# Computing only the chosen experts, with two indirect row gathers for each chosen slot

## The chip, the cores and the metric

The kernel runs on one core of a Trainium2 chip; the other cores are idle. The metric is the device time of one execution in microseconds. The core has a matrix engine (TensorE, PE), a vector engine (DVE), an activation engine (ACT), a general engine (GpSimd, POOL) and SyncE (SP), each with its own instruction queue. Data come from the chip's memory by DMA over 16 DMA engines; SP and POOL issue the transfers here.

## The reference

One layer of an image trunk over 512 latent and 256 context tokens of width 2048, all in fp32: modulation, a token mixer (RG-LRU and RWKV7 halves), a residual with layer norm, and then a PEER mixture of 16,384 experts with a second residual and layer norm. The change touches what follows the mixer:

```python
def peer(h, w_q, sub_keys, u, v):        # u, v: [16384, 2048]
    q = (h @ w_q).reshape(B_, T, 8, 2, 128)
    s = einsum('bthpd,hpkd->bthpk', q, sub_keys)
    s1, i1 = top_k(s[..., 0, :], 16);  s2, i2 = top_k(s[..., 1, :], 16)
    cand_s = s1[..., :, None] + s2[..., None, :]       # 256 per head
    cand_i = i1 * 128 + i2
    top_s, pos = top_k(cand_s, 16);  idx = cand_i[pos]
    gates = softmax(top_s)
    # 8 heads x 16 = 128 chosen experts for each token
    act = gelu(einsum('nkd,nd->nk', u[idx], h))
    return einsum('nk,nkd->nd', gates * act, v[idx])

x = layer_norm(ALPHA * x + gt1 * o_lat, ln1_g, ln1_b)
f = peer(modulate(x, sh2, sc2), ...)
x = layer_norm(ALPHA * x + gt2 * f, ln2_g, ln2_b)
```

## The kernel before, in words

The program is a row of blocks; at the end of each all engines meet, so nothing of one block overlaps the next: `modulation`, `in_projection`, `rglru`, `rwkv`, and `tail` with `out_projection` (its layer norm included), `queries`, `route`, `experts`, `final`. Activations are kept feature-major: a tile has 128 features as partitions and 512 tokens along the row, 16 tiles for the width.

`out_projection` (L1421) ends with a layer norm (L1353) whose matrix product with a constant sums over features on PE. Its finish writes the modulated input of the experts as two fp32r parts, `h_hi` and `h_lo`, and SP stores the normed residual to `x1_dram` in four parts of 1 MB (L1459). `queries` (L1490) leaves, for every token, the 16 best keys and their scores for each of the 16 half-heads in `best_key` and `best_val`.

`route` (L1538) loops over four tiles of 128 tokens. DVE adds the pairs of scores to 256 candidates per head, finds the best 16, works out the two key indices and the softmax gates (L1648 to L1672). Then the chosen gates are spread to a dense matrix: for four tokens at a time DVE builds one-hot rows (L1685), POOL multiplies one of them by the gates (L1581), PE multiplies the two (L1603), ACT copies the product out (L1625), and SP stores 8 MB per tile to `gates_dram` (L1570).

`experts` (L1692) computes all 16,384 experts for all 512 tokens. The work goes in 16 groups of 16 units; a unit is a weight tile of 1 MB, first 8 of the table u, then 8 of the table v. SP loads a unit as soon as both conversions of the tile two units before are done (L1721); ACT makes the high part `ex_hi` (L1738), DVE the low part `ex_lo` (L1752); PE multiplies high by high, high by low and low by high (L1798), 48 matmuls a unit. After each u unit ACT applies Gelu (L1743), DVE multiplies by the gates (L1759) that POOL loads (L1728), and splits the result (L1761, L1763). After each v unit DVE adds two products of 128x512 into the sum `f` (L1769). There are two buffers of each tile.

`final` (L1823) reloads x1 (L1833), scales by the second gate (L1838), adds the residual (L1845) and runs the second layer norm with PE sums (L1378, L1382), ACT's root (L1392, L1394) and SP's four stores (L1854).

Elsewhere in the program, and named by the prediction: `modulation` loads eight weight tiles of 4 MB (L109); `rglru` loads 64 tiles of 1 MB from POOL's queue into three buffers (L479); `rwkv_scan` multiplies by an identity matrix on PE (L1075) to turn tiles.

## Time and profile before

| | |
|---|---|
| median of 3 runs (lowest to highest) | 6884.99 us (6883.69 to 6888.27) |
| the profiled execution's span | 6879.0 us |
| instructions | 80488 |
| PE, DVE, ACT, POOL busy | 6061.1, 2778.5, 1685.7, 366.5 us |
| read from memory, written | 531.84 MB, 61.09 MB |

The profiled execution has no time of its own beside its span; the runs' median stands 6 us above that span. Busy time counts an engine's instructions, not its waits. A granted clock of 1.00 is TensorE at 2.4 GHz and 0.50 at 1.2 GHz; between them a stretch holds both. A DMA share of 1.00 means that all 16 DMA engines had packets all the time. An fp32 matmul of the program stands in the trace as two records, an fp32r one as one.

### The profile page before, as it was taken

What the parts mean: (1) busy time and instruction counts of PE and PEld (TensorE: products, weight loads), DVE (VectorE), ACT (ScalarE), POOL (GpSimd) and SP (SyncE); (2) the same over time, 40 slices, a digit from 0 to 9 for tenths busy, and PEclk for the clock granted to TensorE, in tenths of its full rate; (3) what the DMA queues carried; (4) which work ended last, traced back from release to release, by engine and by line L of the source; (5) the groups of instructions that cost most, each with busy time, mean ns of one, the idle gap of its engine ahead of it and who ended that gap; (6) DMA issues with size and microseconds to landing.
All of it is one profiled execution on the core that took longest, in us unless ns stands there. A gap on an engine that the chain in (4) does not pass through costs nothing. (4 is left out here: it accounts for less than half of the span.)

```text
span 6879.0 us, 80488 instructions
## 1 busy us (share of the span) xinstructions
PE 6061.1 (88%) x32312; PEld 4951.1 (72%) x32312; DVE 2778.5 (40%) x3717; ACT 1685.7 (25%) x1951; POOL 366.5 (5%) x426
## 2 busy tenths in 40 slices
PE   6798988699999999959664569999999999999997
PEld 1687855687788877837453458888888888888885
DVE  1333433443433444232579933333333333333333
ACT  0111225333332333222213312222222222222222
POOL 0000010000000000010003400000000000000000
PEclk8899999788887888769887789999999999999998
DMA  5222275100000000031204353333333333333332
GB/s 227 91 86 82 102 250 182 41 21 11 11 8 8 21 11 11 1 109 61 98 31 79 67 144 110 110 106 107 110 110 110 105 108 108 110 110 106 107 108 86
DMA packets 199453, 595.47 MB, mean 87 GB/s; under 512 B 16884, under 2 KB 121972, under 8 KB 146292
## 3 DMA queue, kind: packets, MB, share of 16 engines
q1 hardware_dynamic: 176160, 477.24, 21.2%
q0 software_dynamic: 22976, 115.63, 5.0%
q8 instruction: 135, 2.21, 0.1%
q14 instruction: 34, 0.28, 0.0%
q10 hardware_dynamic: 148, 0.10, 0.0%
HBM read 531.84 MB, written 61.09 MB: 86 GB/s over the span
## 5 line engine op out<-in xcount | busy, mean ns | idle before, releaser
L1798 PE MATMUL ex_u<-h_hi,ex_hi 128*128 128x512 f32 x2048 | 797.6, 389 | 52.5 <-DVE ex_lo L1752 52.5
L1798 PE MATMUL ex_u<-h_lo,ex_hi 128*128 128x512 f32 x2048 | 797.4, 389 | 0.0
L1798 PE MATMUL ex_u<-h_hi,ex_lo 128*128 128x512 f32 x2048 | 797.3, 389 | 0.0
L1798 PE MATMUL ex_v<-ex_w_hi,ex_hi 128*128 128x512 f32 x2048 | 796.7, 389 | 0.0
L1798 PE MATMUL ex_v<-ex_w_lo,ex_hi 128*128 128x512 f32 x2048 | 796.7, 389 | 0.0
L1798 PE MATMUL ex_v<-ex_w_hi,ex_lo 128*128 128x512 f32 x2048 | 796.7, 389 | 0.0
L1738 ACT ACTIVATE ex_hi<-ex_raw 128x2048 fp32r<-128x2048 f32 x256 | 490.3, 1915 | 1100.8 <-PE ex_v L1798 1100.3
L1752 DVE TENSOR_TENSOR ex_lo<-ex_raw,ex_hi 128x2048 fp32r<-128x2048 f32 x256 | 586.5, 2291 | 84.1 <-ACT ex_hi L1738 84.1
L1769 DVE TENSOR_TENSOR f<-f,ex_v 128x512 f32<-128x512 f32 x256 | 164.5, 684 | 843.1 <-PE ex_v L1798 843.1
L1798 PEld LDWEIGHTS ex_u<-h_hi,ex_hi 128*128 128x128 f32 x2048 | 384.9, 188 | 132.7 <-DVE ex_lo L1752 52.7
L1759 DVE TENSOR_TENSOR ex_w<-ex_act,ex_gates 128x512 f32<-128x512 f32 x128 | 88.7, 693 | 882.2 <-ACT ex_act L1743 882.2
L1798 PEld LDWEIGHTS ex_u<-h_hi,ex_lo 128*128 128x128 f32 x2048 | 384.8, 188 | 80.0
L1798 PEld LDWEIGHTS ex_u<-h_lo,ex_hi 128*128 128x128 f32 x2048 | 384.8, 188 | 79.8
L1798 PEld LDWEIGHTS ex_v<-ex_w_hi,ex_lo 128*128 128x128 f32 x2048 | 384.4, 188 | 79.9
L1798 PEld LDWEIGHTS ex_v<-ex_w_lo,ex_hi 128*128 128x128 f32 x2048 | 384.4, 188 | 79.8
L1798 PEld LDWEIGHTS ex_v<-ex_w_hi,ex_hi 128*128 128x128 f32 x2048 | 384.4, 188 | 79.7
L1743 ACT ACTIVATE ex_act<-ex_u 128x512 f32<-128x512 f32 x128 | 76.8, 600 | 1077.3 <-PE ex_u L1798 1077.3
L994 DVE TENSOR_TENSOR rw_X<-rw_bank,rw_level_mask 128x512 f32<-128x512 f32 x240 | 164.4, 691 | 398.3 <-PE rw_bank L1110 396.9
L250 PE MATMUL pb_acc<-x_hi,pb_hi 128*128 128x512 f32 x832 | 213.0, 338 | 72.8 <-DVE pb_lo L221 72.8
L1685 DVE TENSOR_TENSOR rt_hot<-rt_iota,rt_sel 128x512 f32<-128x512 f32 x256 | 259.1, 1088 | 7.8 <-ACT rt_sel L1617 7.8
L1603 PE MATMUL rt_g<-rt_gated,rt_hot 128*128 128x128 f32 x1024 | 186.1, 339 | 86.2 <-POOL rt_gated L1581 85.2
L605 PE MATMUL late_acc<-lru_late_w,cond_act 128*1 128x128 f32 x2048 | 229.2, 275 | 28.1 <-DMA lru_late_w<-in_ada_late 28.1
(349 smaller groups left out, 9245.2 us busy)
## 6 DMA issues: line engine op xcount, KB each, us to landing
ex_raw<-in_peer_u SPq DMA_DIRECT2D x128, 1024.0 KB, 4.8
ex_raw<-in_peer_v SPq DMA_DIRECT2D x128, 1024.0 KB, 4.8
lru_late_w<-in_ada_late POOLq DMA_DIRECT2D x64, 1024.0 KB, 5.1
ada_w<-in_ada_w SPq DMA_DIRECT2D x8, 4096.0 KB, 20.8
gates_scratch<-rt_dense SPq DMA_DIRECT2D x4, 8192.0 KB, 38.9
ex_gates<-gates_scratch POOLq DMA_DIRECT2D x128, 256.0 KB, 3.0
pb_raw<-in_w_in SPq DMA_DIRECT2D x26, 1024.0 KB, 4.8
pl_raw<-in_w_in SPq DMA_DIRECT2D x18, 1024.0 KB, 4.8
```

The source lines that it names most:

```text
L250: last = nc.tensor.matmul(acc[b][s][:], wt[b][:, ks], x[:, k, c0:c0 + w], start=(k == 0 and n == 0), stop=(k == KT - 1 and n == 2))
L605: last = nc.tensor.matmul(late_acc[rows % 2][part:part + 1, col:col + P], e.cond_act[:, k, 0:1], late_w[n % LATE_BUFS][:, k * P:(k + 1) * ...
L994: nc.vector.tensor_tensor((X if level > 1 else T)[:, 4 * q:4 * q + 4, :], take(("X", level, q))[:].rearrange("p (h n) -> p h n", h=4), mas ...
L1603: ins = nc.tensor.matmul(g_acc[(b * per_turn + f) % 4][:, (n % BANKFUL) * NK:(n % BANKFUL + 1) * NK], hot1[b][:, n, :], gated[b][:, n, :], ...
L1685: ins = nc.vector.tensor_tensor(dst[:], iota[:, None, :].to_broadcast(full), sel[:, m, at, None].to_broadcast(full), ALU.is_equal)
L1738: nc.scalar.activation(hi[u % 2][:], raw[u % 2][:], ACT.Copy).then_inc(hi_done, 1)
L1743: nc.scalar.activation(act_[c % 2][:], u_acc[c % 2][:], ACT.Gelu).then_inc(gelu_done, 1)
L1752: nc.vector.tensor_tensor(lo[u % 2][:], raw[u % 2][:], hi[u % 2][:].bitcast(FP32), ALU.subtract).then_inc(lo_done, 1)
L1759: nc.vector.tensor_tensor(w[c % 2][:], act_[c % 2][:], gates[c % 2][:], ALU.mult).then_inc(weighted, 1)
L1769: nc.vector.tensor_tensor(t, t, v_acc[v % 2][h][:], ALU.add).then_inc(added, 1)
L1798: ins = nc.tensor.matmul(out, wt, x, start=first and n == 0, stop=last and n == 2)
```

## The change

`route`, `experts` and `final` are replaced by one block, `experts`, and a block `token_major` is put between the layer norm and `queries`.

- `token_major` turns the normed residual x1 and the modulated input h2 from feature-major to token-major on PE (32 bank fills of four 128x128 transposes), with ACT and DVE taking the fills in turn; x1 goes to `x1_dram` as one store of 4 MB, h2 stays in SBUF. The four stores of x1 in the layer norm are gone.
- The new `experts` handles 4 token tiles of 128 tokens (tokens are partitions) and 128 chosen slots each: 512 slots. For slot s, each of the 128 tokens has its own expert number. POOL issues an indirect DMA that gathers the 128 rows of 8 KB of table u, and one for table v, each into five buffers of its own, in the order u, v, u, v. The u gather of slot n waits for the dot product of slot n-5, the v gather for PE's use of slot n-5.
- Per slot DVE multiplies the u rows by h2 and sums (one fused instruction over 128x2048, the products written back into the u buffer); ACT applies Gelu to the 128 dots; DVE makes a diagonal matrix of Gelu times gate; PE multiplies it by the v rows, four fp32 matmuls of 128x512, and adds up over the 128 slots of a tile in PSUM. There are four diagonals, and the diagonal of slot n-1 is made behind the dot product of slot n.
- The routing (the part that finds the 16 best pairs and the gates) is cut in ten parts. For tile 0 all stand before the first slot; for the next tile one part stands behind every eighth slot. The dense gate matrix is no longer built. The expert number is written as an integer.
- The second residual and layer norm work on token-major rows, on DVE with `bn_stats`, in two parts at slots 3 and 4 of the next tile; for the last tile after the last slot. The scale and bias rows are broadcast to all partitions at the start.
- The tables u and v are given to the kernel in their own row order. The expert products are plain fp32 without the split in two parts. Loops over groups are gone: the 512 slots are written out.

```diff
...
+        h2 = sb("h2", [P, KT, LAT])
...
-            def on_sp(sp):
-                for q in range(4):
-                    sp.wait_ge(normed, 4 * q + 4)
-                    sp.dma_start(e.x1_dram[:, 4 * q:4 * q + 4, :], z[:, 4 * q:4 * q + 4, :]).then_inc(stored, 16)
-                sp.wait_ge(stored, 64)
...
+        token_major(nc, e, a, z, h2)
...
+def token_major(nc, e, a, x1, h2):
+    with ExitStack() as ctx:
+        sb = lambda n, s, d=FP32: ctx.enter_context(nc.sbuf_tensor("tm_" + n, s, d))
+        ident = sb("ident", [P, P])
+        x1_tok = sb("x1", [P, TOK_TILES, D])
+        banks = [ctx.enter_context(nc.psum_tensor(f"tm_bank{b}", [P, BANK], FP32)) for b in range(8)]
+        ident_loaded, turned, act_taken, dve_taken, stored = sems(
+            nc, ctx, "tm_ident_loaded", "tm_turned", "tm_act_taken", "tm_dve_taken", "tm_x1_stored")
+        fills = [(src, q, t) for src in range(2) for q in range(4) for t in range(TOK_TILES)]
+        dst = (x1_tok, e.h2_tok)
+        with nc.Block() as block:
+            @block.sync
+            def _(sp):
+                sp.dma_start(ident[:], a["ident"]).then_inc(ident_loaded, 16)
+                sp.wait_ge(act_taken, 2 * TOK_TILES)
+                sp.wait_ge(dve_taken, 2 * TOK_TILES)
+                sp.dma_start(e.x1_dram.rearrange("t p d -> p t d"), x1_tok[:]).then_inc(stored, 16)
+                sp.wait_ge(stored, 16)
+            @block.tensor
+            def _(pe):
+                pe.wait_ge(ident_loaded, 16)
+                for n, (src, q, t) in enumerate(fills):
+                    if n >= 8:
+                        pe.wait_ge(dve_taken if n % 2 else act_taken, (n - 8) // 2 + 1)
+                    for j in range(4):
+                        ins = nc.tensor.transpose(banks[n % 8][:, j * P:(j + 1) * P],
+                                                  (x1, h2)[src][:, 4 * q + j, t * P:(t + 1) * P], ident[:])
+                    ins.then_inc(turned, 1)
...
+ROUTE_PARTS = 10
+ROUTE_AT = 6
+ROUTE_EVERY = 8
+FINAL_AT = 3
+SLOTS = PEER_HEADS * TOPK
+BUFS = 5
+DIAGS = 4
...
             @block.sync
             def _(sp):
                 for dst, src in ((ident, a["ident"]), (iota, a["iota"])):
                     sp.dma_start(dst[:], src).then_inc(const_loaded, 16)
+                sp.dma_start(e.gate2_dram.rearrange("o (k p) -> p (o k)", p=P), e.mod[:, 5 * KT:6 * KT, 0],
+                             allow_slow_non_contiguous=True).then_inc(gate2_out, 16)
+                sp.dma_start(rows[:, 1, :], a["ln2_g"].broadcast_to([P, D])).then_inc(rows_loaded, 16)
+                sp.dma_start(rows[:, 2, :], a["ln2_b"].broadcast_to([P, D])).then_inc(rows_loaded, 16)
+                sp.wait_ge(gate2_out, 16)
+                sp.dma_start(rows[:, 0, :], e.gate2_dram.broadcast_to([P, D])).then_inc(rows_loaded, 16)
+                for t in range(TOK_TILES):
+                    if t:
+                        sp.wait_ge(x1_used, t)
+                    sp.dma_start(x1[:], e.x1_dram[t]).then_inc(x1_loaded, 16)
+                    if t:
+                        sp.wait_ge(normed, t)
+                        sp.dma_start(out[t - 1], z[:]).then_inc(out_stored, 16)
+                sp.wait_ge(normed, TOK_TILES)
+                sp.dma_start(out[TOK_TILES - 1], z[:]).then_inc(out_stored, 16)
+                sp.wait_ge(out_stored, 16 * TOK_TILES)
             @block.gpsimd
             def _(pool):
+                def gather(n, table, rows, loaded):
+                    t, s = n // SLOTS, n % SLOTS
+                    pool.indirect_dma_start(rows[n % BUFS][:], None, table,
+                                            bass.IndirectOffsetOnAxis(expert[:, t, s:s + 1], 0)).then_inc(loaded[n % BUFS], 16)
+                for n in range(total_slots):
+                    if n % SLOTS == 0:
+                        pool.wait_ge(chosen_ready, n // SLOTS + 1)
+                    if n >= BUFS:
+                        pool.wait_ge(dotted, n - BUFS + 1)
+                    gather(n, a["peer_u"], u_row, u_loaded)
+                    if n >= BUFS:
+                        pool.wait_ge(slot_used, n - BUFS + 1)
+                    gather(n, a["peer_v"], v_row, v_loaded)
             @block.tensor
             def _(pe):
+                for n in range(total_slots):
+                    t, s = n // SLOTS, n % SLOTS
+                    if s == 0 and t >= 2:
+                        pe.wait_ge(x1_used, t - 1)
+                    pe.wait_ge(v_loaded[n % BUFS], 16 * (n // BUFS + 1))
+                    pe.wait_ge(diag_ready, n + 1)
+                    for c in range(D // BANK):
+                        ins = nc.tensor.matmul(f_acc[t % 2][:, c * BANK:(c + 1) * BANK], diag[n % DIAGS][:],
+                                               v_row[n % BUFS][:, c * BANK:(c + 1) * BANK], start=s == 0, stop=s == SLOTS - 1)
+                    ins.then_inc(slot_used, 1)
             @block.scalar
             def _(act):
+                def exponent(t):
...
+                act.wait_ge(scratch_ready, 1)
+                exponent(0)
+                for n in range(total_slots):
+                    t, s = n // SLOTS, n % SLOTS
+                    act.wait_ge(dotted, n + 1)
+                    nc.scalar.activation(gelu[:, t, s:s + 1], dots[:, t, s:s + 1], ACT.Gelu).then_inc(gelu_done, 1)
+                    if t + 1 < TOK_TILES and s == ROUTE_AT + EXP_PART * ROUTE_EVERY:
+                        exponent(t + 1)
+                    if t and s == FINAL_AT:
+                        root(t - 1)
+                root(TOK_TILES - 1)
             @block.vector
             def _(dve):
+                c = Chain(dve, v_step)
+                fc = Chain(dve, f_step)
+                def route(t, part):
...
+                    if part in (1, 2, 3):
+                        best_part(nc, c, landed, top, pos, cand, left, PEER_HEADS, part - 1)
+                    if part == 4:
...
+                def dot(n):
+                    t, s, b = n // SLOTS, n % SLOTS, n % BUFS
+                    dve.wait_ge(u_loaded[b], 16 * (n // BUFS + 1))
+                    nc.vector.tensor_tensor_reduce(out=u_row[b][:], in0=u_row[b][:], in1=e.h2_tok[:, t, :], op0=ALU.mult, op1=ALU.add,
+                                                   scale=1.0, scalar=0.0, accum_out=dots[:, t, s:s + 1]).then_inc(dotted, 1)
+                def weigh(n):
+                    t, s = n // SLOTS, n % SLOTS
+                    dve.wait_ge(gelu_done, n + 1)
+                    if n >= DIAGS:
+                        dve.wait_ge(slot_used, n - DIAGS + 1)
+                    nc.vector.tensor_scalar(diag[n % DIAGS][:], ident[:], gelu[:, t, s:s + 1], gate[:, t, s:s + 1], ALU.mult, ALU.mult
+                                            ).then_inc(diag_ready, 1)
+                def finish(t, part):
+                    acc = f_acc[t % 2]
+                    if part == 0:
+                        dve.wait_ge(slot_used, (t + 1) * SLOTS)
+                        dve.wait_ge(rows_loaded, 48)
+                        if t:
+                            dve.wait_ge(out_stored, 16 * t)
+                        fc.ordered(nc.vector.tensor_tensor(z[:], acc[:], rows[:, 0, :], ALU.mult))
+                        dve.wait_ge(x1_loaded, 16 * (t + 1))
+                        nc.vector.scalar_tensor_tensor(out=z[:], in0=x1[:], scalar=ALPHA, in1=z[:], op0=ALU.mult, op1=ALU.add
+                                                       ).then_inc(x1_used, 1)
+                        dve.wait_ge(x1_used, t + 1)
+                        for q in range(4):
+                            ins = nc.vector.bn_stats(stats[:, q, :], z[:, q * BANK:(q + 1) * BANK])
+                        fc.ordered(ins)
+                        nc.vector.bn_aggr(mv[:], stats[:].rearrange("p q s -> p (q s)")).then_inc(var_ready, 1)
+                    if part == 1:
+                        dve.wait_ge(rstd_ready, t + 1)
+                        fc.ordered(nc.vector.tensor_scalar(z[:], z[:], mv[:, 0:1], rstd[:], ALU.subtract, ALU.mult))
+                        fc.ordered(nc.vector.tensor_tensor(z[:], z[:], rows[:, 1, :], ALU.mult))
+                        nc.vector.tensor_tensor(z[:], z[:], rows[:, 2, :], ALU.add).then_inc(normed, 1)
...
+                for part in range(ROUTE_PARTS):
+                    route(0, part)
+                for n in range(total_slots):
+                    t, s = n // SLOTS, n % SLOTS
+                    dot(n)
+                    if n:
+                        weigh(n - 1)
+                    if t and s in (FINAL_AT, FINAL_AT + 1):
+                        finish(t - 1, s - FINAL_AT)
+                    part, off = divmod(s - ROUTE_AT, ROUTE_EVERY)
+                    if t + 1 < TOK_TILES and off == 0 and 0 <= part < ROUTE_PARTS:
+                        route(t + 1, part)
+                weigh(total_slots - 1)
+                finish(TOK_TILES - 1, 0)
+                finish(TOK_TILES - 1, 1)
```

## Rows read from the trace of the kernel before

**Rows 1.** The page, part 1: busy time, share of the span, instructions.
```profile
PE 6061.1 (88%) x32312; PEld 4951.1 (72%) x32312; DVE 2778.5 (40%) x3717; ACT 1685.7 (25%) x1951; POOL 366.5 (5%) x426
```

**Rows 2.** Busy time by stage (us busy, x instructions), then granted clock, DMA share, GB/s.
```profile
core 0: us, PE busy (x) PEld busy (x) DVE busy (x) ACT busy (x) POOL busy (x), PEclk, DMA share, GB/s
3548.00:4003.00 455.00, 189.68 (x1036) 161.49 (x1036) 391.43 (x589) 138.17 (x136) 166.22 (x128) 0.70 0.37 74
4003.00:6802.00 2799.00, 2787.40 (x12288) 2307.57 (x12288) 979.04 (x896) 594.82 (x416) 70.25 (x128) 1.00 0.32 108
6802.00:6879.00 77.00, 30.93 (x64) 11.47 (x64) 37.54 (x68) 23.89 (x36) 0.00 (x0) 0.75 0.29 110
```

**Rows 3.** Groups of the expert stage: count | busy us, mean ns | idle before, releaser.
```profile
L1798 PE MATMUL ex_u<-h_hi,ex_hi 128*128 128x512 f32 x2048 | 797.6, 389 | 52.5 <-DVE ex_lo L1752 52.5
...
L1752 DVE TENSOR_TENSOR ex_lo<-ex_raw,ex_hi 128x2048 fp32r<-128x2048 f32 x256 | 586.5, 2291 | 84.1 <-ACT ex_hi L1738 84.1
```

**Rows 4.** SP's issues in order of time, from the end of the queries on.
```profile
3548.03 0.34 SPq L1565 DMA_DIRECT2D rt_ident<-in_ident  x1
...
4075.61 75.84 SPq L1721 DMA_DIRECT2D ex_raw<-in_peer_v  x8
...
4249.68 75.85 SPq L1721 DMA_DIRECT2D ex_raw<-in_peer_v  x8
```

**Rows 5.** Waits, 4070 to 6840 us: us in total, times, longest.
```profile
ACT ex_hi L1738 <- PE ex_v L1798: 1100.3, 126, 9.0
```

**Rows 6.** DVE in order of time, routing of token tile 0.
```profile
3548.29 0.06 DVE L1637 MEMSET rt_landed<- 128x2 f32 x1 [2.18 <-PEq L79]
...
3556.09 0.08 DVE L1483 MATCH_VALUE_LOAD rt_pos<-rt_top,rt_score 128x8 f32 x1
...
3562.51 0.15 DVE L1477 COPY rt_landed<-rt_landed 128x1 f32<-128x1 f32 x1
...
3584.44 0.29 DVE L1672 TENSOR_TENSOR rt_chosen<-rt_chosen,rt_total 128x128 f32<-128x128 f32 x1
```

**Rows 7.** DMA issues: count, KB each, median us from issue to landing.
```profile
lru_late_w<-in_ada_late POOLq DMA_DIRECT2D x64, 1024.0 KB, 5.1
...
x_scratch<-z SPq DMA_DIRECT2D x4, 1024.0 KB, 3.8
...
out_dram<-f SPq DMA_DIRECT2D x4, 1024.0 KB, 4.3
```

**Rows 8.** Busy time, clock and DMA of three stretches with loads queued together.
```profile
885.00:893.00 8.00, 2.15 (x11) 1.28 (x12) 3.34 (x20) 0.00 (x0) 0.00 (x0) 0.50 1.04 418
903.00:923.00 20.00, 14.39 (x122) 10.16 (x120) 19.55 (x22) 0.00 (x0) 2.16 (x4) 0.91 1.02 386
20.00:70.00 50.00, 50.00 (x129) 11.28 (x128) 0.33 (x2) 1.76 (x3) 0.00 (x0) 1.00 1.01 434
```

**Rows 9.** Single lines: duration in ns, minimum/median/maximum.
```profile
L479 POOL DMA_DIRECT2D lru_late_w<-in_ada_late x64: 540/540/551, 883.0 to 1153.4; - x64
...
L1581 POOL TENSOR_TENSOR rt_gated<-rt_hot,rt_sel x128: 1040/1307/1312, 3588.2 to 3959.3; 128x512 f32<-128x512 f32 x128
...
L1685 DVE TENSOR_TENSOR rt_hot<-rt_iota,rt_sel x256: 676/688/1529, 3586.7 to 3957.6; 128x512 f32<-128x512 f32 x128
...
L1759 DVE TENSOR_TENSOR ex_w<-ex_act,ex_gates x128: 691/693/695, 4027.8 to 6715.1; 128x512 f32<-128x512 f32 x128
```

**Rows 10.** TensorE's fp32 products: chain, group, and stretches at either clock.
```profile
6820.52 15.60 PE ln_mean L1378 x32
...
L1075 PE MATMUL rw_bank<-rw_ident,rw_v 128*128 128x128 f32 x96 | 15.1, 310 | 0.0
...
6820.00:6823.00 3.00, 2.48 (x3) 1.17 (x4) 0.17 (x2) 0.00 (x0) 0.00 (x0) 0.50 0.08 11
3610.00:3620.00 10.00, 7.19 (x40) 6.11 (x40) 10.00 (x11) 5.12 (x5) 6.34 (x5) 0.84 0.00 0
```

**Rows 11.** ACT at the end: a table load before the root of the variance.
```profile
6851.73 1.28 ACT L1392 ACT_TABLE_LOAD   x1
```

More of the change, by code:

```diff
@@ L1547, in route @@
         k12, k12_f = sb("k12", [P, 2, P], U32), sb("k12_f", [P, 2, P])
[L1548 removed]
+        chosen = sb("chosen", [P, 2, P])
         total, landed = sb("total", [P, PEER_HEADS]), sb("landed", [P, 2])
[L1550 to L1553 removed]
@@ L1559, in route @@
-        tiles, turns, fills = LAT // P, P // SPREAD, P // BANKFUL
-        per_turn = SPREAD // BANKFUL
+        expert_f = sb("expert_f", [P, P])
+        expert, gate = sb("expert", [P, TOK_TILES, SLOTS], U32), sb("gate", [P, TOK_TILES, SLOTS])
+        dots, gelu = sb("dots", [P, TOK_TILES, SLOTS]), sb("gelu", [P, TOK_TILES, SLOTS])
+        u_row = [sb(f"u{b}", [P, D]) for b in range(BUFS)]
+        v_row = [sb(f"v{b}", [P, D]) for b in range(BUFS)]
+        diag = [sb(f"diag{b}", [P, P]) for b in range(DIAGS)]
@@ new lines, in experts @@
+        dotted, gelu_done, diag_ready, slot_used = sems(nc, ctx, "dotted", "gelu_ready", "diag_ready", "slot_used")
+        x1_loaded, x1_used, normed, out_stored, var_ready, ln_done, rstd_ready = sems(
+            nc, ctx, "ex_x1_loaded", "ex_x1_used", "ex_out_normed", "ex_out_stored", "ex_var_ready", "ex_ln_done", "ex_rstd_ready")
+        u_loaded = sems(nc, ctx, *[f"u{b}_loaded" for b in range(BUFS)])
+        v_loaded = sems(nc, ctx, *[f"v{b}_loaded" for b in range(BUFS)])
+        total_slots = TOK_TILES * SLOTS
@@ L1884, in tail @@
             out_projection(nc, e, a)
-            with ExitStack() as picks:
-                e.best_key, e.best_val = (picks.enter_context(nc.sbuf_tensor(n, [P, TOK_TILES, HP, TOPK], FP32))
-                                          for n in ("best_key", "best_val"))
-                queries(nc, e, a)
-                route(nc, e, a)
-            f = inner.enter_context(nc.sbuf_tensor("f", [P, KT, LAT], FP32))
-            experts(nc, e, a, f)
-            final(nc, e, a, f, out)
+            queries(nc, e, a)
+        experts(nc, e, a, out)
 def position_tables():
```

372 lines of the change are left out of this document (98 added, 274 removed).

## The prediction

> **What bounds the kernel now.** I read the page's busy times first, then the busy time by stage, then the waits of the longest stage. [rows 1] shows TensorE (PE) busy for 88% of the span; that is an average, so the stages come next. [rows 2] cuts off the part that the change replaces: from 3548 to 4003 us the gate matrix is built (`route`, 455 us), from 4003 to 6802 all 16,384 experts are computed (2799 us, PE busy 2787 of them at clock 1.00, DMA share only 0.32), and from 6802 to 6879 stands the last normalisation (77 us). In the expert stage everything waits for PE: ACT's conversion of the next weight tile waits 1100 us for the products [rows 5]. A group of 16 weight tiles starts every 4249.68 - 4075.61 = 174.07 us [rows 4]; 16 groups are 2785 us, 768 matmuls of 0.227 us in each (2048 of each of six kinds [rows 3]). DVE (979 us) and ACT (595 us) have room. So the stage is 12,288 matmuls long, and its weights (268 MB) cost nothing. The whole tail is 6879 - 3548 = 3331 us; what stands before 3548 keeps its code but for one insertion.
>
> **What goes.** The 3331 us of [rows 2], with the 8 MB gate stores and the reload.
>
> **What comes, in order of time.**
>
> *token_major, new, between the layer norm and the queries.* 32 fills of four fp32 transposes each, 128 in all. A transpose-like 128x128 matmul against the identity took 15.1/96 = 0.157 us of PE [rows 10]; the x1 half is 64 x 0.157 = 10 us. The copies out (16 on each of ACT and DVE, 0.6 to 0.7 us) lie beside PE. SP then stores x1, 4 MB, and the block ends when it has landed: one 1 MB store took 3.8 us [rows 7], four at the full rate below some 12. The h2 half of the transposes hides beside that store. Identity load 2.5, transposes 10, last copy 0.7, store 12, block ends 1.5: 27 us (bounds: 20, if all but the second half is hidden, and 45, if PE stays at half clock and the store goes at 3.8 us a MB after another). The four x1 stores removed from the layer norm gave no wait that ends it, so nothing comes back.
>
> *The first routing, exposed.* DVE's chain for tile 0 ran from 3548.29 to 3584.7 in the kernel before [rows 6]; it stands unchanged (TENSOR_TENSOR and reduce at 2.29 us each) plus two small casts: 37.5 us. The other three tiles' routing is cut in ten parts between slots and lies beside transfers. Start of the gathers: 3548 + 27 + 37.5 = 3612.5 us.
>
> *512 slots.* Each brings two gathers of 128 rows of 8 KB, 2 x 1,048,576 B, against 268 MB in all before: 1074 MB. Per slot the resources need:
> - DMA: POOL-issued loads of 1 MB with 8 KB rows ran at 418 GB/s, with share 1.04, when three were queued together; over 903 to 923, mixed with SP's loads, 386; 4 MB loads with 32 KB rows 434 [rows 8]. No row shows rows picked at random, nor an indirect issue. Random places can lose some of the rate but gain nothing; bounds: 434, and below the 206 GB/s of one load at a time (1 MB in 5.1 us from issue to landing [rows 7]). With five buffers for each table up to ten gathers can be in flight, so the overlapped rows are the nearest; I take 418: 2,097,152 B / 418 = 5.02 us.
> - PE: four fp32 matmuls 128x512; each stands as two records. The 16 such products of a layer norm are 32 records in 15.60 us [rows 10], 0.49 us a record with its cold start; 8 records are 3.9 us.
> - DVE: the dot product reads two 128x2048 tiles, 2.29 us as the subtraction of that shape [rows 3], the diagonal some 0.2. The routing of a tile is 37 us, its finish 16: (37 + 16)/128 = 0.4 a slot. Together 2.9 us. The fused multiply-and-sum is in no row; bounds 2.29 and, if it runs twice, 4.6: both under 5.02.
> - ACT: one 128x1 Gelu, under 0.4; its table changes (1.28 us each [rows 11]) come a few times a tile.
> - POOL: two indirect issues. A direct one of 1 MB took 0.540 us [rows 9]. An indirect one must also read its 128 indices; POOL's only two-input operation, 128x512, took 1.31 [rows 9]. Bounds 0.54 and 2.3 (if it is held back by a whole dot product); I take 1.3, so 2.6 a slot. Behind a waiting gather stands the gather of the other table, in one queue.
>
> DMA is the longest: 512 x 5.02 = 2569 us. Is the queue ever empty? The v buffer of slot n comes free after the dot of n+1 (DVE is in order, and the diagonal of n stands behind it), that is 5 + 2.5 us after u of n landed, and PE's 3.9: about 11.5 us. Five slots are 25 us, so 13 us of transfers stay queued. Routing parts of up to 6.4 us (the search and replace part, 3556.09 to 3562.51 in [rows 6]) fit under that; the two finish parts (about 8 us each, at neighbouring slots) nearly don't. For three tile ends and the ramp I add 20 us (0 to 60).
>
> *The ends.* First gather: 5.1 us to landing less 2.5 of transfer = 2.6 us. Last: when the last v row has landed, Gelu and diagonal 0.7, PE 3.5 to 3.9, then the finish: five DVE passes over 128x2048 at 2.29 (11.5), the statistics 2.5, two ACT table loads at 1.28 with their operations (3, partly beside), then the 1 MB store, 4.3 [rows 7]: 25 us together after overlap. The old finish of 77 us had its layer norm through PE; that is in what goes.
>
> **The sum.** 3612.5 + 2.6 + 2569 + 20 + 25 = 6229 us of span. The profiled execution's span is 6879.0 and the median of the runs 6885.0, so 6 us lie around it: 6235, which I round to **6240 us**. Saved are 230 us of expert stage, 455 - 37.5 of routing and 52 of the end, less 27 for token_major and 20 for gaps.
>
> In [rows 8] a loaded HBM stream reaches 418 to 434 GB/s. The Trainium skill, page "DMA: Bandwidth & Descriptors", section "Specifications", gives about 358 GB/s as the HBM limit of one core. The trace does not agree while the other core is idle (434 measured); by 358 a slot would be 5.86 us and the time about 6670, which lies inside rival 1 below.
>
> **Rivals.**
> 1. *The gather is slower than a plain load, yet still what bounds.* For it: scattered 8 KB rows are in no row here; the mixed stretch gave only 386. Against: rows that are contiguous in themselves are what both queues move today, and both reach share 1.0. At 386: 5.43 us, 2782, in all 6450; at 340: 6825.
> 2. *POOL becomes the bound, and the kernel slower.* Mechanism: POOL reads the indices from SBUF while DVE holds the read path for its two-input dot. The row for it: DVE's 128x512 two-input operation took 0.69 us alone (0.691 to 0.695 in the expert stage) but up to 1.53 in `route`, where POOL's two-input operation ran beside it, itself 1.04 to 1.31 [rows 9]. So they do hold each other up. If no issue can go beside dot and diagonal, a slot is 2.5 + 2 x issue. With 1.3 that is 5.1, no change. The kernel gets slower from (6879 - 3660)/512 = 6.29 us a slot, an issue of 1.9 us; at 2.0 a slot is 6.5, in all 6994. Against: the u gather is released by the end of a dot, when DVE has only 0.2 us to do and then idles until the next row lands.
> The Trainium skill, page "SBUF — State Buffer", section "Who interferes with whom", says it the same way: a DVE operation with two SBUF inputs contends with a GpSimd instruction that reads SBUF, as a lock on the whole instruction. Whether an indirect DMA is such an instruction no row shows.
> 3. *POOL or the buffers bound, but below that point* (5.2 to 6.2 us a slot): 6330 to 6840.
> 4. *PE's clock.* At granted clock 0.5 a layer-norm record took 0.83 us (three in 2.48 us [rows 10]), so a slot would need 6.6 us, above DMA: 3379, in all 7045. For it: PE idles in every slot. Against: in `route` PE was 72% busy, in bursts, and had 0.84 [rows 10]; here it would be 78%, at 0.84 still 4.1 to 4.6 us. And a PE that is late is busy all the time, which went with 1.00 [rows 2].
>
> **How the numbers follow.** Forecast (DMA bound, 400 to 434 GB/s) 0.60, own range 6140 to 6370; rival 1 below that rate 0.18; rival 2 0.10; rival 3 0.08; rival 4 0.03; no change 0.01. Low end: 434 GB/s and no gaps, 3612.5 + 2.6 + 2474 + 25 + 6 = 6120. High end: in rivals 1 and 3 to about 6.1 us a slot, 6800; what is left out are rivals 2 and 4 and little below. Faster by over 0.2% (about what a measurement here tells from no change): 0.60 + 0.18 + 0.08 = 0.86; within 0.2% 0.01; slower 0.13.
>
> **What would show it.** Right: DMA share near 1.0 and 400 GB/s or more from about 3615 us on; u and v landing every 5.0 us; POOL waiting for `dotted` or `slot_used`; DVE idle before each dot, ended by a DMA; PE 70 to 80% busy; token_major about 27 us between the layer norm and the first query load. Rival 1: share 1.0, but below 400 GB/s. Rivals 2 and 3: share clearly under 1, POOL never idle, its indirect issues longer than 1.9 us or of two lengths, one the shorter by a dot. Rival 4: records of 0.8 us and DVE waiting for `slot_used`. The forecast is wrong if slots stand further apart than 5.3 us.

## The result, and the profile after

The changed kernel takes 6192.46 us (median of 4 runs, 6190.14 to 6200.88) against 6886.63 us (4 runs, 6883.69 to 6897.67) for the kernel before: ratio 0.8992, 95% interval [0.8979, 0.9005]. The forecast was 6240 with a range of 6120 to 6800. The profiled execution took 6200.88 us, with a span of 6199.2. It is the slowest of the four, 8.4 us above their median, so the steps below are read inside it, from one stage start to the next.

The page after: busy times, then the rows of the 40 slices (155 us each) for PE, granted clock, DMA and GB/s.

```profile
PE 4988.4 (80%) x23148; PEld 3246.0 (52%) x23148; DVE 2875.9 (46%) x4099; ACT 1067.8 (17%) x1921; POOL 1347.0 (22%) x1194
...
PE   7699889678999999999595947777777777777776
...
PEclk9899999878878788877697979999999999999999
DMA  5222247400000000000321269999999999999997
GB/s 239 96 84 77 103 157 248 145 29 23 12 12 8 9 12 12 12 12 1 114 74 69 75 281 427 427 427 427 423 427 427 423 426 427 427 426 427 427 427 333
```

Against [rows 1], PE falls from 88 to 80%, but the line that explains the time is DMA's: 9 in every slice from 3720 us on but the last. The longest busy row and the bound are no longer the same engine. Busy time by stage (us busy, x instructions, granted clock, DMA share, GB/s) answers [rows 2]: routing of tile 0, filling of the buffers, two stretches of slots, the end.

```profile
3590.00:3628.00 38.00, 0.00 (x0) 0.00 (x0) 33.59 (x85) 1.59 (x2) 2.22 (x3) 0.50 0.33 117
3628.00:3640.00 12.00, 0.88 (x1) 0.50 (x2) 4.86 (x5) 0.41 (x2) 9.86 (x8) 0.50 1.00 416
3640.00:4200.00 560.00, 423.78 (x912) 167.93 (x910) 323.78 (x425) 25.80 (x116) 270.12 (x228) 0.98 1.01 427
...
4960.00:6150.00 1190.00, 890.50 (x1920) 350.93 (x1920) 658.03 (x815) 55.89 (x248) 562.04 (x481) 0.99 1.01 427
...
6165.00:6199.00 34.00, 10.78 (x24) 4.39 (x24) 16.53 (x17) 3.47 (x6) 0.00 (x0) 0.75 0.08 35
```

DMA share 1.01 and 427 GB/s through the slots, where [rows 2] had 0.32 and 108. PE is busy for 76% of the time (423.78/560). The waits of 3640 to 6150 us (us in total, times, longest) say the same from the engines' side:

```profile
POOL ex_v L1563 <- PE ex_f L1585: 1102.5, 469, 9.7
DVE ex_u L1662 <- DMA ex_u<-in_peer_u,ex_expert: 1076.8, 469, 3.8
PE ex_f L1585 <- DVE ex_diag L1670: 690.7, 462, 65.4
```

DVE waits for rows before nearly every dot product; POOL waits for a free v buffer, which is room in hand, not a stall, as long as the rows already asked for keep the transfers going. (The longest wait of PE, 65.4 us, is its first one, most of it ahead of the gathers.)

One slot, in order of time (start, us, what, idle before it and its releaser):

```profile
4508.27 0.94 POOL L1563 DMA_INDIRECT ex_v<-in_peer_v,ex_expert  x1 [3.55 <-PE ex_f L1585]
4509.24 2.29 DVE L1662 CUSTOM_DVE_ANT_0 ex_u<-ex_u,h_tok 128x2048 f32<-128x2048 f32 x1 [2.37 <-DMA ex_u<-in_peer_u,ex_expert]
4509.51 2.83 POOL L1563 DMA_INDIRECT ex_u<-in_peer_u,ex_expert  x1 [0.30 <-issue]
...
4512.65 0.94 POOL L1563 DMA_INDIRECT ex_v<-in_peer_v,ex_expert  x1 [0.30 <-issue]
4513.89 0.94 POOL L1563 DMA_INDIRECT ex_u<-in_peer_u,ex_expert  x1 [0.30 <-issue]
4514.13 2.29 DVE L1662 CUSTOM_DVE_ANT_0 ex_u<-ex_u,h_tok 128x2048 f32<-128x2048 f32 x1 [2.33 <-DMA ex_u<-in_peer_u,ex_expert]
...
4516.83 3.67 PE L1585 MATMUL ex_f<-ex_v,ex_diag 128*128 128x512 f32 x8 [1.22 <-DVE ex_diag L1670]
```

Dots start 4.89 us apart, which is 2,097,152 B at 429 GB/s. The dot product takes 2.29 us: the fused multiply-and-sum is one pass. The slot whose u rows land at 4509.24 gives its v buffer back at 4516.83 + 3.67 = 4520.50, 11.3 us later: its diagonal stands behind the next dot, and PE's product behind the diagonal. The issues show the contention of rival 2: alone 0.94 us, but the one that begins at 4509.51, inside a dot that ends at 4511.53, takes 2.83 and ends 0.81 us after the dot. One that began 0.24 us before a dot (4513.89) was not held. All issues of 3640 to 6150 (ns, minimum/median/maximum):

```profile
L1563 POOL DMA_INDIRECT ex_v<-in_peer_v,ex_expert x507: 932/1347/3022, 3639.8 to 6149.8; - x169
L1563 POOL DMA_INDIRECT ex_u<-in_peer_u,ex_expert x506: 933/937/2982, 3641.1 to 6146.6; - x169
```

The landmarks of the new path, from SP's and POOL's timelines: token_major from its first load to the first load of the queries, the start of the expert block, and the first gather.

```profile
3338.22 0.33 SPq L1404 DMA_DIRECT2D tm_ident<-in_ident  x1
3350.66 0.38 SPq L1407 DMA_DIRECT2D x_scratch<-tm_x  x1
3362.87 0.33 SPq L1471 DMA_DIRECT2D q_keys<-in_peer_keys  x1
...
3588.28 0.34 SPq L1541 DMA_DIRECT2D ex_ident<-in_ident  x1
```
```profile
3625.17 1.03 POOL L1563 DMA_INDIRECT ex_u<-in_peer_u,ex_expert  x1 [565.94 <-DVE ex_expert L1656]
```

And the last transfers (clock, DMA share, GB/s at the end of each row), with the last dot product, the last two slots on PE, the first operation of the finish and the last store:

```profile
6160.00:6161.00 1.00, 0.37 (x1) 0.30 (x2) 0.48 (x3) 0.20 (x1) 0.00 (x0) 1.00 0.97 410
...
6163.00:6164.00 1.00, 1.00 (x4) 0.23 (x2) 1.00 (x1) 0.00 (x0) 0.00 (x0) 1.00 0.14 57
6164.00:6170.00 6.00, 3.97 (x9) 1.44 (x8) 3.63 (x6) 0.20 (x1) 0.00 (x0) 1.00 0.06 25
6170.00:6171.00 1.00, 0.56 (x2) 0.35 (x3) 0.64 (x4) 0.91 (x2) 0.00 (x0) 1.00 0.00 0
```
```profile
6167.74 2.29 DVE L1662 CUSTOM_DVE_ANT_0 ex_u<-ex_u,h_tok 128x2048 f32<-128x2048 f32 x1 [2.37 <-DMA ex_u<-in_peer_u,ex_expert]
...
6170.44 7.10 PE L1585 MATMUL ex_f<-ex_v,ex_diag 128*128 128x512 f32 x16 [1.25 <-DVE ex_diag L1670]
6177.59 2.29 DVE L1680 TENSOR_TENSOR ex_z<-ex_f,ex_rows 128x2048 f32<-128x2048 f32 x1 [6.93 <-PE ex_f L1585]
...
6192.91 0.34 SPq L1556 DMA_DIRECT2D out_dram<-ex_z  x1
```

### The profile page after: what moved, and what is told of

It reads as the page before. It is cut to its first block and busy times, and to the rows that moved or that the text cites. A ratio compares the mean times of both kernels' runs of the same rounds, so it can differ in the third digit from the quotient of the medians.

```text
span 6199.2 us, 59084 instructions
## 1 busy us (share of the span) xinstructions
PE 4988.4 (80%) x23148; PEld 3246.0 (52%) x23148; DVE 2875.9 (46%) x4099; ACT 1067.8 (17%) x1921; POOL 1347.0 (22%) x1194
## 5 line engine op out<-in xcount | busy, mean ns | idle before, releaser
L1585 PE MATMUL ex_f<-ex_v,ex_diag 128*128 128x512 f32 x4096 | 1906.9, 611 | 696.9 <-DVE ex_diag L1670 696.9
L1585 PEld LDWEIGHTS ex_f<-ex_v,ex_diag 128*128 128x128 f32 x4096 | 753.2, 193 | 1849.9 <-issue 1849.8
L1662 DVE CUSTOM_DVE_ANT_0 ex_u<-ex_u,h_tok 128x2048 f32<-128x2048 f32 x512 | 1173.4, 2292 | 1096.6 <-DMA ex_u<-in_peer_u,ex_expert 1095.4
L1563 POOL DMA_INDIRECT ex_v<-in_peer_v,ex_expert x512 | 696.6, 1361 | 1158.4 <-PE ex_f L1585 1104.8
L1563 POOL DMA_INDIRECT ex_u<-in_peer_u,ex_expert x512 | 520.1, 1016 | 721.7 <-DVE ex_expert L1656 565.9
L1058 PE MATMUL rw_bank<-rw_X,rw_Tt 128*128 128x128 f32 x1920 | 253.6, 275 | 0.0
L1058 PE MATMUL rw_bank<-rw_Tt,rw_X 128*128 128x128 f32 x1920 | 253.6, 275 | 0.0
L1045 PEld LDWEIGHTS rw_bank<-rw_T,rw_Mb 128*128 128x128 f32 x1920 | 244.0, 209 | 12.9 <-issue 11.6
L1045 PE MATMUL rw_bank<-rw_T,rw_Mb 128*128 128x128 f32 x1920 | 249.9, 293 | 0.0
L1058 PEld LDWEIGHTS rw_bank<-rw_X,rw_Tt 128*128 128x128 f32 x1920 | 233.7, 192 | 0.0
```

The source lines that it names most:

```text
L1045: ins = nc.tensor.matmul(out[:, j * C:(j + 1) * C], Mb[:, sl, 0, :], ident[:] if level == 1 else T[:, sl, :], start=True, stop=True)
L1058: ins = nc.tensor.matmul(out[:, j * C:(j + 1) * C], first[:, sl, :], second[:, sl, :], start=True, stop=True)
L1563: pool.indirect_dma_start(rows[n % BUFS][:], None, table, bass.IndirectOffsetOnAxis(expert[:, t, s:s + 1], 0)).then_inc(loaded[n % BUFS], 16)
L1585: ins = nc.tensor.matmul(f_acc[t % 2][:, c * BANK:(c + 1) * BANK], diag[n % DIAGS][:], v_row[n % BUFS][:, c * BANK:(c + 1) * BANK], start= ...
L1662: nc.vector.tensor_tensor_reduce(out=u_row[b][:], in0=u_row[b][:], in1=e.h2_tok[:, t, :], op0=ALU.mult, op1=ALU.add, scale=1.0, scalar=0.0 ...
```

## The experiments

All are edits of the changed kernel. Theory A is the prediction's: the bytes of the rows at the full rate set the time, and POOL, DVE, PE and the buffers only have to stay under 4.9 us a slot. Outside of the 512 slots it leaves 6192 - 512 x 4.91 = 3678, about 3680 us; slot times below are (time - 3680)/512.

**Half the bytes of v.** Rows of v of 4 KB, each half used twice; the sum over v's second half is left out.

```
-        v_row = [sb(f"v{b}", [P, D]) for b in range(BUFS)]
+        v_row = [sb(f"v{b}", [P, D // 2]) for b in range(BUFS)]
```

> Only the first 1024 columns of the v rows are gathered (4 KB a row) and PE uses them twice, so the second half of each expert's output is left out; all instruction counts stay. Theory A (the 16 DMA engines bound the slots at about 427 GB/s): a slot brings 1.573 MB instead of 2.097, 3.68 us instead of 4.91, just above PE's 3.5 to 3.7; slots every 3.7 to 3.9 us, in all 5560 to 5680 us. Theory B (POOL's two issues, held up by the dot product, set the pace): the number of issues is the same, no change, 6190 us. Theory C (PE with its idle clock sets the pace): no change either.

Measured 5663.01 us (2 runs), ratio 0.8217 [0.8200, 0.8233]: 529 us less for 268 MB less. In 4000 to 5000 us:

```profile
4000.00:5000.00 1000.00, 921.23 (x2017) 374.84 (x2016) 734.14 (x946) 65.57 (x268) 780.25 (x505) 0.98 0.99 401
```

The bytes bound the changed kernel, as theory A said (5560 to 5680 us). A slot is now 3.87 us, and the next limits are near: PE 92% busy, and POOL at 780 us with 157 more of gaps between back-to-back issues. The run also shows rival 2's formula to be too high: two issues of 0.94 beside no dot would give 2.5 + 1.88 = 4.4 us a slot.

**Rows in order, and one input to the dot.** The first takes the rows p + 128 s in place of the chosen experts; the second sums u's row alone, without h2, at the same 2.29 us of DVE.

```
+                        c.ordered(nc.vector.tensor_scalar(expert_f[:], in_order[:], 0.0, None, ALU.add))
```
```
-                    nc.vector.tensor_tensor_reduce(out=u_row[b][:], in0=u_row[b][:], in1=e.h2_tok[:, t, :], ...
+                    nc.vector.tensor_reduce(dots[:, t, s:s + 1], u_row[b][:], AX, ALU.add).then_inc(dotted, 1)
```

> The expert number of slot s on partition p is 128*s + p for every token tile, so each gather reads 1 MB that lies in one piece; which experts are applied is therefore not what the reference says. Theory A with no price for scattered rows: 427 GB/s as before, the same time within 0.3%, 6175 to 6210 us. Rival (scattered 8 KB rows lose some of the rate): the 434 GB/s of the plain 4 MB loads or more, a slot 4.83 us, 6150 us or less.

Measured 6196.27 us (6193.32 to 6199.54), ratio 0.8989 [0.8974, 0.9004], 426 GB/s: scattered rows of 8 KB cost nothing here.

> The dot product is replaced by a plain sum over the u row: one SBUF input instead of two, about the same 2.29 us of DVE; the multiplication by h2 is left out. If the two-input read is what holds POOL's issues, the v issue's median falls from 1.35 to 0.94 us and none is longer than about 1.0. Theory A: the time stays within 0.3%, 6175 to 6210 us, since DMA binds. Theory B (the held issues cost the stream something): faster by more, up to 0.4 us a slot, down to 5990 us.

Measured 6185.86 us (6180.97 to 6197.13), ratio 0.8981 [0.8966, 0.8996], the same time within the intervals. Its issues in 4000 to 5000 us:

```profile
L1563 POOL DMA_INDIRECT ex_v<-in_peer_v,ex_expert x201: 932/936/1246, 4000.2 to 4996.2; - x101
```

The median issue of a v row falls from 1.35 to 0.94 us. The edit takes away two things, the second input and the writing of 128x2048 products back over the u rows, and does not tell them apart. The changed kernel's own trace does. The first operation of the finish writes as much, but has only one input in SBUF (`ex_f` lies in PSUM), and the issue that begins inside it is not held; it ends before the operation does:

```profile
4916.50 2.28 DVE L1680 TENSOR_TENSOR ex_z<-ex_f,ex_rows 128x2048 f32<-128x2048 f32 x1
...
4917.43 0.93 POOL L1563 DMA_INDIRECT ex_u<-in_peer_u,ex_expert  x1 [0.31 <-issue]
```

So what holds an issue is the dot's second input from SBUF, as rival 2 said, and under the transfers it costs nothing. (Single issues of u rows still reached 2.60 us in the run with one input: they begin inside DVE's routing operations with two inputs in SBUF, which are unchanged in it.)

**POOL loaded until it bounds.** A memset of 128x2048, 1.82 us, before each gather, and 4 buffers to make room.

```
+                    pool.wait_ge(pool_step, 2 * n + (table is not a["peer_u"]))
+                    nc.gpsimd.memset(spare[:], 0.0).then_inc(pool_step, 1)
```

> POOL fills a spare tile of 128x2048 (1.8 us) ahead of each gather; four buffers instead of five, to make room. The prediction's rival 2 in its own formula (no issue can go beside dot and diagonal, slot = 2.5 + 2 x issue, with 1.8 + 0.94 an issue): 8.0 us a slot, 7770 us. Theory A (POOL is off the path until its own work is longer than 4.9 us a slot, and only the part of an issue that overlaps a dot is held up): 2 x (1.8 + 0.94 + 0.3) = 6.1 us plus up to 0.8 for held issues, 6.1 to 6.9 us a slot, 6800 to 7220 us. If POOL's time did not matter at all: 6190 us.

Measured 7412.43 us (2 runs), ratio 1.0755: 7.29 us a slot. POOL:

```profile
4506.31 0.94 POOL L1567 DMA_INDIRECT ex_v<-in_peer_v,ex_expert  x1 [0.16 <-POOL ex_spare L1566]
4507.25 1.82 POOL L1566 MEMSET ex_spare<- 128x2048 f32 x1
4509.23 2.96 POOL L1567 DMA_INDIRECT ex_u<-in_peer_u,ex_expert  x1 [0.16 <-POOL ex_spare L1566]
4512.19 1.83 POOL L1566 MEMSET ex_spare<- 128x2048 f32 x1
```

The dot of that slot began at 4509.09. Two memsets and their gaps are 3.96 us, one free issue 0.94, one held issue up to 2.96: 7.9. Counted over the trace, one issue is held in 388 of the 512 slots, both in 11 and none in 113; with the mean issues of 4000 to 5000 us, 2.35 us (u) and 1.01 us (v), the sum is 7.32. When POOL bounds, the issue of u comes due as the dot runs, again and again: that is rival 2's mechanism, and it makes this kernel slower than the kernel before. Without held issues the same work would be 3.96 + 2 x 0.94 = 5.84 us a slot, an estimate of some 6670 us in all. Both forecasts missed: A's range (6800 to 7220) took shorter holds, and the rival's formula, with both issues outside of the dot, gave 7770.

**DVE loaded.** Each dot done twice, with 4 buffers.

```
+                    fc2.ordered(nc.vector.tensor_tensor_reduce(out=spare[:], in0=u_row[b][:], in1=e.h2_tok[:, t, :], ...
```

> Each dot product is done twice (the second into a spare tile), with 4 buffers in place of 5 to make room: two two-input reads of 2.29 us a slot. Theory A (what an engine does under the transfers costs nothing until it passes 4.9 us a slot): DVE needs 2 x 2.29 + 0.34 + 0.4 to 0.5 of routing and finish, 5.35 us a slot, and is just above the transfers: 3683 + 512 x 5.35 = 6420 us (6390 to 6500), DVE busy all the time, DMA share about 0.92. Rival 2 (POOL's two issues get through only when DVE holds no two-input read): 4.6 us of reads and two issues of 0.94 are 6.5 to 6.9 us a slot, 7000 to 7200 us, POOL's issues 3 us and more each.

Measured 6452.1 us (2 runs), ratio 0.9362 [0.9344, 0.9381]: 5.41 us a slot, DVE busy 927 of 1000 us, DMA share 0.95. POOL's median issues were 2.16 us (u) and 1.45 (v), 678 us in 1000; both issues of a slot were held in 384 of the 512 slots, yet POOL was not the bound. A's sum of 6420 us holds to 32 us; it counted nothing for the change to four buffers, which alone, below, cost 30.

**The buffers.** `BUFS = 5` set to 2, 3 and 4.

> BUFS is 2 instead of 5 (two buffers of u rows, two of v rows). Theory A (the transfers bound, and buffers only have to cover a loop): a freed v buffer lets POOL issue v of slot n and behind it u of slot n+1 (1 us each), they land some 6 us later behind each other, then comes the dot of n+1 (2.3), the diagonal of n (0.35) and PE's products of n (3.7), which free the buffer for n+2: two slots in about 14.4 us, 7.2 us a slot. All that lies outside of 512 slots is 6192 - 512 x 4.9 = 3683 us, so 7370 us (6750 to 7420 for slots of 6.0 to 7.3 us), DMA share about 0.6 to 0.8, POOL waiting for PE. Rival (the row traffic keeps itself going with any two buffers, since a queue of two is never empty): 6192 us.

> BUFS is 3 instead of 5. Theory A: the same loop of some 14.4 us now covers three slots, 4.8 us a slot, just at the 4.9 us that the transfers need: 6190 to 6290 us, DMA share 0.97 to 1.0. Rival B (the loop is longer than A adds up, since the issues are held by dots and the rows land behind ten others): slots of 5.5 us or more, 6500 us or more. If A's loop holds, five buffers hold two in reserve.

> BUFS is 4 instead of 5. With 2 buffers a slot took 8.75 us and with 3 it took 5.90, so the loop from the issue of a u row to the release of its v buffer is 17.5 to 17.7 us, when PE is idle in it and at the lower clock. Theory A (slot = the longer of 4.9 us and loop / buffers): 17.6 / 4 = 4.4, under 4.9, so 6192 us (6185 to 6215, the upper end for the routing parts that hold a dot back). Rival (the loop grows with the rows in flight, as a row waits behind more others): 5.2 us a slot or more, 6350 us or more.

Measured: 2 buffers 8160.83 us, ratio 1.1842 [1.1817, 1.1866]; 3 buffers 6712.7, ratio 0.9740 [0.9721, 0.9760]; 4 buffers 6221.93 (6210.95 to 6223.54), ratio 0.9026 [0.9007, 0.9046]. Slots of 8.75, 5.92 and 4.96 us. Theory A's first two expectations were too low: the loop is 17.5 us for 2 and 17.8 for 3, not 14.4, and with 3 buffers the rival (6500 us or more) came true. With 2 buffers the loop can be read on POOL, DVE and PE:

```profile
4502.65 0.94 POOL L1563 DMA_INDIRECT ex_v<-in_peer_v,ex_expert  x1 [11.97 <-PE ex_f L1585]
4503.89 0.93 POOL L1563 DMA_INDIRECT ex_u<-in_peer_u,ex_expert  x1 [0.30 <-issue]
...
4511.78 2.29 DVE L1662 CUSTOM_DVE_ANT_0 ex_u<-ex_u,h_tok 128x2048 f32<-128x2048 f32 x1 [10.25 <-DMA ex_u<-in_peer_u,ex_expert]
...
4514.49 8.68 PE L1585 MATMUL ex_f<-ex_v,ex_diag 128*128 128x512 f32 x16 [8.68 <-DVE ex_diag L1670]
```

The u row lands 7.9 us after its issue, where 6 was reckoned. PE, idle for 8.68 us before, is then slow for the first products: 8.68 us for two slots, against 7.10 for the last two of the changed kernel. The granted clock is 0.57 from 4514.49 to 4518.20 and 1.00 after that, and the mean granted clock of 4000 to 5000 us is 0.77 (0.88 with 3 buffers, 0.98 with 5). The v buffer is given back at 4520.01, 5.5 us after the products began; 3.7 was reckoned. A shortage of buffers thus makes its own loop longer. Four buffers need 17.6/4 = 4.4 us and come within 0.5% of five, though 7 us above the range that was expected (6185 to 6215). What they lose goes where routing parts hold dots back: 3670 to 4000 us, with routing, ran at 419 GB/s, and 4080 to 4240, without, at 427; with five buffers both ran at 427.

**One gather a slot.** u and v side by side in one table, rows of 16 KB.

```
-                    gather(n, a["peer_v"], v_row, v_loaded)
+                    gather(n, a["peer_uv"], uv_row, u_loaded)
```

> u and v stand side by side in one table of rows of 16 KB, and each slot has one gather of 2 MB in place of two of 1 MB; five buffers of 16 KB. POOL issues half as often, a row is twice as long, the bytes are the same. Theory A (the transfers bound): within 0.3% of the changed kernel, 6175 to 6210 us; DMA share near 1.0 at 427 GB/s; POOL's busy time about half. Rival C (two gathers a slot cost something at the queue, or rows of 8 KB lose rate): the rate rises from 427 towards 434 GB/s (the rate of the plain 32 KB rows in the kernel before), 6150 us or less. Against both: the u buffer is now held as long as the v buffer, and the dot begins only when both rows have landed; if that counted, over 6250 us.

Measured 6200.84 us (6190.6 to 6211.76), ratio 0.8999 [0.8982, 0.9017]; 426 GB/s, POOL busy 269 us in 1000 where it was 481. Half the issues and twice the row length move neither rate nor time.

**What is exposed ahead of the gathers.** The first tile is routed in four units of two heads; the gathers start after the first. The unaltered kernel ran beside it.

```
+UNITS = [(0, 0, 2), (0, 2, 4), (0, 4, 6), (0, 6, 8), (1, 0, 8), (2, 0, 8), (3, 0, 8)]
+NEEDED = {0: 0, 32: 1, 64: 2, 96: 3, 128: 4, 256: 5, 384: 6}
-                    if n % SLOTS == 0:
-                        pool.wait_ge(chosen_ready, n // SLOTS + 1)
+                    if n in NEEDED:
+                        pool.wait_ge(chosen_ready, NEEDED[n] + 1)
```

> The changed kernel unaltered, beside the two others of this set: 6192 us, within 0.2%. It is the base that they are read against.

> The first token tile is routed in four units of two heads each instead of all eight at once: the gathers start when the first 32 slots are known, and the other three units, as well as those of the later tiles, are routed in parts between slots. Each operation on a unit of two heads is a quarter as wide. Also, the diagonal of slot 510 is made before the dot of slot 511. Theory A (all that lies ahead of the first gather is added to a row traffic of fixed length): the first unit needs about 11 us where the first tile needed 36.9, 26 us less: 6192 - 26 = 6166 us (6155 to 6175). Rival (the routing parts between the first slots keep DVE behind by as much as the early start gains, or the ramp is bound by DVE rather than by the transfers): 6185 to 6200 us, with a DMA share under 0.9 in the first 150 us of the gathers.

Measured: unaltered 6197.48 us (5 runs, 6190.47 to 6203.87), ratio 0.8995 [0.8978, 0.9011]; routed in units 6183.14 (6177.2 to 6188.36), ratio 0.8973 [0.8958, 0.8989]. The ranges do not overlap, but the intervals of the ratios do; so the traces decide. From the expert block's first load to the end of the span the changed kernel took 6199.2 - 3588.28 = 2610.9 us, unaltered again 2611.4, in units 6186.6 - 3590.78 = 2595.8: 15 us gained, 26 expected, and the time lies between the two ranges that were expected (6155 to 6175, 6185 to 6200). (The two traces of the unaltered kernel differ by 0.5 us here.) The first gather comes 13.9 us after the block's start instead of 36.9, 23 us earlier. But from it to the start of the last dot are 2551.7 us, and 2542.6 in the changed kernel: 9 us are given back, and 1.5 us are gained behind it by making the diagonal of slot 510 first. The rows show to whom. The changed kernel, then the one in units:

```profile
3600.00:3612.00 12.00, 0.00 (x0) 0.00 (x0) 11.79 (x44) 1.59 (x2) 0.00 (x0) 0.50 0.80 334
3612.00:3625.17 13.17, 0.00 (x0) 0.00 (x0) 12.58 (x10) 0.00 (x0) 0.00 (x1) 0.50 0.00 1
```
```profile
3592.00:3604.69 12.69, 0.00 (x0) 0.00 (x0) 10.69 (x37) 1.51 (x2) 0.00 (x0) 0.50 0.32 44
3604.69:3624.00 19.31, 0.00 (x0) 0.00 (x0) 4.42 (x3) 0.20 (x1) 12.53 (x11) 0.50 1.00 423
```

Four loads of 1 MB (two layer norm rows, gate row, x1) come after a store of the gate row in numbers of 4 bytes. SP issues the first two right behind the store, and they do not get through beside it; for the other two the program itself waits for the store, which takes 11.9 us (3589.14 to 3601.07 in the changed kernel). There the four still fit under the routing (334 GB/s, then 0); here 4.06 MB of them, by the queue's row for 3600 to 3660, move beside the first gathers: 9.5 us at 427 GB/s. The last run takes that store out of the way:

```
                sp.dma_start(ident[:], a["ident"]).then_inc(ident_loaded, 16)
+                sp.dma_start(e.gate2_dram.rearrange("o (k p) -> p (o k)", p=P), e.mod[:, 5 * KT:6 * KT, 0],
+                             allow_slow_non_contiguous=True).then_inc(gate2_out, 16)
```

> The kernel with the first tile routed in units, and one move more: the store of the gate row to DRAM (2048 single numbers of 4 bytes) goes from the start of the expert block into token_major, where it lies beside the transposes. In the kernel before this one (routed in units) that store held up the four 1 MB loads behind it (two layer norm rows, the gate row, x1) until 3604 us, so that 4.06 MB of them moved during the first gathers, where the unaltered version had moved them while it routed. Theory A (every byte that moves beside the gathers is added at the full rate: 4.06 MB at 427 GB/s are 9.5 us): the four loads now run from 3592 to 3602, before the first gather, and 9 us more come back: 6183 - 9 = 6174 us; in the profile the expert block, from its first load to the end of the span, lasts 2587 us where it lasted 2596. Rival (the 9 us are lost at the ramp by PE at its lower clock or by the filling of the buffers, whatever else is transferred): 6180 to 6186 us, the block 2594 to 2598 us. A rival in token_major: the small store delays the 4 MB store of x1 by its own 10 us, and nothing is gained in all.

Measured 6184.43 us (5 runs, 6176.18 to 6185.2), ratio 0.8974 [0.8962, 0.8986]: 10 us above theory A's 6174, inside the rival's 6180 to 6186, and by the times alone not to be told from the run before. Blocks ahead of this one differ by more than that from run to run, so the block is read by itself. By the trace, one for each kernel, it took 6175.3 - 3585.91 = 2589.4 us, 6.4 less, and first gather to last dot 2545.5, 6.2 less:

```profile
3586.00:3599.79 13.79, 0.00 (x0) 0.00 (x0) 10.78 (x39) 1.51 (x2) 0.00 (x1) 0.50 0.77 314
3599.79:3619.00 19.21, 4.69 (x6) 2.12 (x7) 7.80 (x9) 0.42 (x3) 14.36 (x11) 0.50 0.91 363
```

The loads now run under the routing. token_major kept its 24.6 us. Two thirds of the 9.5 us came back, so theory A holds for that part; 2.9 us of the slots are not accounted for. Both versions beat the kernel before and, by their traces, the changed kernel, the second by 21.5 us of block.

## Why the prediction was right

The mechanism held: DMA bound at full share, nothing else behind it, and the runs above bear it out: fewer bytes shorten the slots, while the order of the rows, their length, the number of gathers and the held issues do not change them. The term that was mis-sized is that of the slots.

- *Ahead.* In the profiled run everything up to the layer norm ran 13.7 us later than in the kernel before, in code that the change does not touch (its first load stood at 3239.91 there, at 3253.61 here, and between 3241.0 and 3263.0 in the experiments): this is mostly spread from run to run, and the execution of the kernel before with the span of 6879.0 was a quick one, at 6880.55 us. The layer norm and the queries took 1.9 us more, token_major 3362.87 - 3338.22 = 24.6 us (27 predicted), the exposed routing 36.9 (37.5). The first gather was issued at 3625.17, predicted 3612.5: +12.7.
- *Slots.* Predicted 2.6 + 2569 + 20 = 2591.6 us from the first issue to the last landing; measured 6170 - 3625.17 = 2545, 47 less. The rate was 427 GB/s and not 418 (512 x 2,097,152 B / 427 = 2515 us, 54 less than the term), and 30 us remain for ramp, tile ends and the slow last landing, where 2.6 + 20 were allowed. The truth lay between two rates of [rows 8], 434 and 418: with 434 the term would have been 2474 us, 41 too short, and with 418 it was 54 too long. The 418 was misread as POOL's own: from 882 to 896 us SP's queue, with small packets, moved 2.55 MB beside POOL's 3.05 MB, so that this stretch was mixed too, and it was 8 us long. A dip at a tile end is small: 411 GB/s over 40 us. What sets 427 and not more is open.
- *End.* From the last landing 29 us, 25 predicted. The diagonal of slot 510 stands behind the dot of 511, so PE had two slots left, 7.10 us, and not one. Making it first cut dot-to-finish from 9.9 to 8.4 us in the kernel with units.
- *Sum.* 6229 + 12.7 - 47 + 4 = 6199 us of span, measured 6199.2. The median of the runs is 8.4 us below the profiled execution, which itself took 1.7 us more than its span, where 6 us were added. So of the 43 us between 6235 and the measured 6192, the slots are 47, and the rest nearly cancels: 12.7 and 4 one way, 8.4 and 4.3 the other.
- *PE.* 3.67 us a slot (3.9 predicted) at clock 0.98. Rival 4 did not come about with five buffers, but with two PE did slow down in its idle loop.
- *POOL.* Issues of 0.94 us alone, 1.0 and 1.36 on average (1.3 taken). Rival 2's mechanism is real (0.94 to 3.02 us, gone with one input), and the loaded run shows where it decides. Its price was overstated: only an issue that begins inside a dot is held, and only to 0.8 us after the dot's end. In the changed kernel that was one issue in 455 of the 512 slots and both in 13, mostly v's, which met the end of a dot (449 of 512, median 1.35 us). The u issue was hardly held (32, median 0.94), as forecast, but not for the reason given: it starts 0.30 us behind the v issue ahead of it, not at the end of a dot.
- *Rival 1.* It did not come about: 427 GB/s, and rows in order and chosen rows have the same rate. Whether the 7 GB/s below the plain loads' 434 belong to the indirect issue was not tried. By the Trainium skill, page "DMA: Bandwidth & Descriptors", section "Specifications", about 358 GB/s would be one core's limit; the trace does not agree: 427 over 2500 us, with the other cores idle, is above it for far longer than the 434 over 50 us that stood in [rows 8].
- *Rival 3.* It did not come about with five buffers. The v buffer was freed 11.3 us after the landing of u (11.5 predicted), but that is not the whole loop. With two buffers a row took 7.9 us from issue to landing, and from issue to release the loop was 17.5 us. "13 us of transfers stay queued" left the way from issue to landing out: five buffers cover 24.5 us of transfers, 1.4 times the loop, and three fall short. (With five, a row lands 15.9 us after its issue in the median, most of it spent behind rows asked for before it.)

## What to carry over

When a change swaps products for transfers, the time is bytes over rate, and what other engines do under it is free until one of them passes the slot. Look at what else moved in the stretch from which the rate is taken, prefer long stretches, and keep the spread: here neither 418 nor 434 was right, and the term was off by some 2% with either. Count buffers by the whole loop, issue, queue, landing, use and release, and look at the granted clock in it: with two buffers TensorE idled, and its part of the loop grew from 3.7 to 5.5 us. Once transfers bound, work is gained only ahead of the first one and behind the last, and loads moved into the bound stretch are paid for byte by byte.

## What was not expected of the hardware

- Indirect gathers of 128 rows ran at 427 GB/s for 2500 us, the same for rows of 8 KB at random, 8 KB in order, and 16 KB. With half of the gathers at 4 KB the rate was 401 at share 0.99; part of that may be POOL's, and the run does not separate it.
- An indirect issue costs POOL 0.94 us and is held until 0.8 us after the end of an operation of DVE with two inputs in SBUF in which it begins. In the run with the loaded POOL a one-input TENSOR_SCALAR of 128x2048 held one too (1.73 us, all three that began in one) and itself took 3.53 us beside POOL's memset, where it takes 1.34 alone.
- The DMA engines do not finish together. From 6164 to 6170 us the share is 0.06, that of one engine of 16, and the last dot waited for it, while the others had ended by about 6164. The last dots still began 4.9 us apart (6157.92, 6162.81, 6167.74), so this engine kept the pace of the slots (25 GB/s, where 427/16 is 26.7) and was only behind. What makes it late was not tried.
- A store of 2048 numbers of 4 bytes took 11.9 us. Two loads of 1 MB issued within 1.5 us behind it landed 14.6 and 16.0 us after their issue; with the store moved away and four loads in the same place, 314 GB/s moved there, where the kernel with units had 44.
